# Two gated heads side by side on 64 partitions each: the scores of a forgetting attention, their masks, and a projection cut at 384

## The chip, the core and the metric

One NeuronCore of a Trainium2 chip runs the whole program. The metric is the device time of one execution in microseconds (us); lower is better. The kernel is written by hand for the five engines: TensorE (PE: matmuls; PEld: its weight loads), VectorE (DVE), ScalarE (ACT), GpSimd (POOL) and SyncE (SP, which issues the DMAs).

## The reference, cut to what matters

512 tokens of width 1024 go through a transformer block with a "forgetting" attention, then through two more blocks, one with a differential attention (DA), one with a latent attention (MLA). All is fp32. The parts that the change touches:

```python
# forgetting attention: 8 heads of 64, in four query blocks i of 128
logits = einsum(q[:, :, q0:q1], k[:, :, :q1])             # q times 64 ** -0.5
logits = logits + c[:, :, q0:q1, None] - c[:, :, None, :q1] # c: cumsum of log forget gates
logits = where(s_pos <= t_pos, logits, -inf)              # causal, token by token
p = softmax(logits); out = p @ v[:, :, :q1]
# DA: 8 heads, each with two maps of 64; mask by chunks of 64 tokens
a = p[:, :, 0] - lam * p[:, :, 1]
# MLA: 16 heads; keys of 64 + 32 columns; mask by chunks of 64 tokens
proj = h @ w_in                   # 1024 -> 384 (q latent) + 256 (kv latent) + 32
sc = (einsum(q_nope, k_nope) + einsum(q_pe, k_pe)) * scale
```

## The kernel before

**Numbers as two parts.** Every fp32 operand is split into a high and a low part (tensors `R`, `WH`, `WL`, `KT`, `PT`), and each product is three matmuls: high by high, low by high, high by low.

**Order.** The host program describes each strand of work as a Python generator. `run()` picks the next step again and again: it estimates from `takes()` when each engine is free and when each operand is ready, and emits the step that can begin first. The order it finds is fixed in the program; on the chip each engine works through its own list in that order and waits on semaphores. Weights are loaded by SP into `RAW` (2 buffers), split by ACT (`whi`) and DVE (`wlo`) into 3 slots, and used by `gemm_f` and `gemm_t`.

**Forgetting scores (fg).** Two groups `A0`, `A1` of four heads. `attention(..., "fg", 2)` makes 32 units (head, query block i), of nk = 128, 256, 384 or 512 keys. A unit's step `score` has five matmuls over all 128 partitions (lines 1747 to 1753): three products of 2 heads' queries (128 rows) with one head's keys. `k_tiles` puts each head's keys in the upper or lower 64 rows of a tile of its own, and the other 64 rows are zeros (`k_zero`: 16 memsets on POOL at the start), so that the other head's queries add nothing. The fourth (line 1752) adds the gates: `gate_rows` places high and low parts of c in every fourth row by 4 DMAs, `gate_cq` and `key_row` (one per head, 8) copy them on ACT. The fifth (line 1753) adds the mask: `IDR` (identity) times `MASK_C`. The bank in PSUM then goes through `max` (DVE), `exp` (ACT), `p_one` (DVE), `turn` (PE transposes, line 1664), `hi`/`lo`, and `values` (PE, lines 1659 to 1661).

**DA scores.** `score_two` has both maps of a head: queries and keys of map 0 lie in partitions 0 to 63, those of map 1 in 64 to 127. Each matmul takes 64 partitions (lines 1761, 1763), two after each other into two banks, and so for three products and the mask. There are 32 such steps, one for each head and query block.

**MLA scores.** Sixteen heads of four blocks, 64 units of `score` with 96 partitions and no gate. Their mask matmul (line 1753) is `HALF` times `MASK_H`, both of 128 partitions and 128 columns, where the two halves of the partitions hold the same rows.

**Latents.** `gemm_t(NM.X, 8, 512, ...)` and `gemm_t(NM.X, 8, 160, ...)` make the 672 columns of MLA's first projection: for each of 8 slices of 128 inputs and 4 blocks of tokens, three matmuls of 512 columns, then three of 160 (lines 1688 to 1690). `turn_lat(0..3)` wait for the first four results, `turn_lat(4)`, the squares of the kv latent and `kpe` for all eight.

Of the kernel before, what the change touches and what calls it, by code (L numbers as in the profile page):

```python
# [5 lines left out]
P = 128  # L6
# [13 lines left out]
C_ID, C_MA, C_MC, C_IH, C_ONE = 0, 128, 256, 384, 512  # L20
C_SEL = 640
C_BASE = 648
C_CDA, C_SDA = 650, 682
C_CML, C_SML = 714, 778
C_WF = 842
C_END = 906
# [17 lines left out]
    "vec": {"pe": 1, "act": 1}, "cvec": {"pe": 1, "act": 1}, "consts": {"act": 1}, "k_zero": {"pool": 1}, "blank": {"pool": 1},  # L44
# [5 lines left out]
    "key_row": {"act": 1}, "score": {"pe": 1}, "score_two": {"pe": 1}, "max": {"dve": 1}, "exp": {"act": 1},  # L50
# [87 lines left out]
def takes(kind, eng, f):  # L138
# [9 lines left out]
    if eng == "pe":  # L148
        if kind == "gemm_f":
            return 3 * len(f["xs"]) * mm(512)  # L150
        if kind == "warm":
            return 430.0
        if kind == "gemm_t":
            return 3 * len(f["xs"]) * mm(f["width"])
        if kind == "mix":
            return 3 * mm(512)
        if kind == "score":
            return (3 if f["gate"] is None else 4) * mm((f["i"] + 1) * P) + 62
        if kind == "score_two":
            return 3 * max(220.0, 1.1 * mm((f["i"] + 1) * P)) + 200  # L160
# [36 lines left out]
    return {"acc": 1595.0, "window": 1250.0, "kpe_copy": 1130.0, "k_zero": 520.0, "ramp": 220.0}.get(kind, 120.0)  # L197

def build(nc, a, out):  # L200
    with ExitStack() as ctx:
# [11 lines left out]
        RC = sb("RC", [P, 512], F32R)  # L213
# [17 lines left out]

        IDR, MASK_C, MASK_H, HALF = (RC[:, n * P:n * P + P] for n in range(4))

# [22 lines left out]
        strands, ready_at, free_at = [], {}, dict.fromkeys(LAG, 0.0)  # L256
# [7 lines left out]
        def emit(kind, **fields):  # L264
            t = None
            for eng, n in SIGNALS[kind].items():
# [33 lines left out]
        def run():  # L300
            while strands:
# [22 lines left out]
                s = min((x for x in can if x[1] == eng and x[0] <= t + PATIENCE[eng]), key=lambda x: x[2].rank)[2]  # L324
# [402 lines left out]
        def landing(s, t):  # L727
# [7 lines left out]
        k_zeros = [emit("k_zero", lo=64 if hh % 2 == 0 else 0, i=s * 8 + hh * 2 + x).pool  # L735
                   for s in range(2) for hh in range(4) for x in range(2)]
        kfree = [[k_zeros[-1]] for _ in range(16)]
# [105 lines left out]
        def k_tiles(base):  # L843
            def put(n, bank, done):
                parts, his = [(base + (2 * n + x) * 2, slice(64 * x, 64 * x + 64)) for x in (0, 1)], []
                for i, r in parts:
                    st = yield step("hi", dst=KT[r, i, :], src=bank[r, :], scale=1.0, after=counts([done, kfree[i], kfree[i + 1]]))
                    his.append(st.act)
                for (i, r), hi in zip(parts, his):
                    st = yield step("lo", dst=KT[r, i + 1, :], src=bank[r, :], high=KT[r, i, :], scale=None, from_x=False, after=[hi])  # L850
                    kready[i] = [st.dve]
                return [st.dve]
            return put

# [10 lines left out]
        def attention(groups, kind, lag):  # L865
            nh = 2 if kind == "da" else 4
            krows = 96 if kind == "mla" else P
            mask = (IDR, MASK_C) if kind == "fg" else (HALF, MASK_H)
            units = [(G, h, i) for G in groups for h in range(nh) for i in range(4)]
# [4 lines left out]
            def key_rows(G, h, u):  # L874
                while u > state.scored + 2 or not (flags.consts and G.gated) or not tiles.fr:
                    yield None
                ck = tiles.get()
                st = yield step("key_row", dst=R[:, ck.i, :], src=G.ck, head=G.h0 + h, after=counts([ck.free, G.ck_done]))
                ck.ready = [st.act]
                G.ckh[h] = ck  # L880

            def one_map(L, u, c, b, scored):
                G, h, i = units[u]
                nk, o = (i + 1) * P, u % STN * 8
                nm, z = ST[:, o + c:o + c + 1], ST[:, o + 2 + c:o + 3 + c]
                mx = yield step("max", dst=nm, src=BK[b.i][:, 0:nk], after=[scored])
# [3 lines left out]
                L.p[c], L.p_done[c] = p, ex.act  # L890

            def unit(u):
                G, h, i = units[u]
                nk, maps = (i + 1) * P, 2 if kind == "da" else 1
                while state.scored < u or u > state.turned + lag or not (G.turned and G.gated and flags.consts and h < G.heads):
                    yield None
                ck = None
                if kind == "fg":
                    while h not in G.ckh:
                        yield None  # L900
                    ck = G.ckh[h]
                L = Group()
                L.p, L.p_done = [None] * maps, [None] * maps
                bs = []
                for c in range(maps):
                    b = yield from bank()
                    bs.append(b)
                if kind == "da":
                    q, kidx = G.Q[h], G.kbase + 4 * h
                    st = yield step("score_two", banks=[b.i for b in bs], q=(q.h.i, q.l.i), kidx=kidx, i=i,  # L910
                                    after=counts([*[b.free for b in bs], q.ready, kready[kidx]]))
                    for c, b in enumerate(bs):
                        spawn(one_map(L, u, c, b, st.pe))
                else:
                    (b,) = bs
                    q = G.Q[h // 2 if kind == "fg" else h]
                    kidx = G.kbase + 2 * h
                    gate = None if ck is None else (G.cq.i, ck.i)
                    more = [] if ck is None else [ck.ready, G.cq.ready]
                    st = yield step("score", bank=b.i, q=(q.h.i, q.l.i), kidx=kidx, i=i, rows=krows, gate=gate, mask=mask,  # L920
                                    after=counts([b.free, q.ready, kready[kidx], *more]))
                    spawn(one_map(L, u, 0, b, st.pe))
                state.scored = u + 1
                if i == 3:
                    if kind == "fg":
                        tiles.put(ck, st.pe)
                    if kind != "fg" or h % 2:
                        drop(q, st.pe)
                while None in L.p_done:
                    yield None  # L930
                o = u % STN * 8
                z, rz = ST[:, o + 2:o + 2 + maps], ST[:, o + 4:o + 4 + maps]
                p1 = FS[:, L.p[0].i, 0:nk]
                if maps == 1:
                    st = yield step("p_one", z=z, rz=rz, p=p1, after=L.p_done)
                else:
                    p2, nl = FS[:, L.p[1].i, 0:nk], ST[:, o + 6:o + 7]
                    while G.nlam is None:
                        yield None
                    st = yield step("p_two", z=z, rz=rz, p1=p1, p2=p2, nl=nl, nlam=G.nlam, after=L.p_done)  # L940
                    fsl.put(L.p[1], st.dve)
# [4 lines left out]
                st = yield step("turn", bank=b.i, src=FS[:, L.p[0].i, 0:nk], i=i, odd=odd, after=counts([b.free, st.dve]))  # L946
                state.turned = u + 1
                fsl.put(L.p[0], st.pe)
# [7 lines left out]
            def values(n):  # L956
# [4 lines left out]
                odd = h % 2  # L961
                pair = G.O[h if kind == "da" else h // 2]
# [3 lines left out]
                at_v = h if kind == "da" else h // 2  # L966
                vs = [(G.V[j // 2].h.i, G.V[j // 2].l.i, (j % 2) * 256 + at_v * P) for j in range(4)]
# [3 lines left out]
                if h == nh - 1:  # L971
# [5 lines left out]
                O = BK[b.i]  # L977
                if kind == "da":
                    ev, sq = (yield from fslot()), (yield from fslot())
                    squared = yield step("o_sq", dst=FS[:, sq.i, 0:S], bank=b.i, after=counts([st.pe, sq.free]))  # L980
# [1240 lines left out]
```

## Time and profile before

| | us |
|---|---|
| median of 3 runs | 1829.36 (1827.6 to 1829.54) |
| the profiled execution, whole | 1828.21 |
| its span, from the first to the last instruction | 1826.4 |
| PE busy in the span | 1808.6 (99%), 8960 matmuls |
| DVE / ACT / POOL busy | 1121.5 / 799.3 / 145.2 |

The granted TensorE clock is 0.999 of full speed over the span. The forgetting scores lie between 68 and 141 us, the DA scores between 619 and 797, the latents' projection between 1210 and 1246, MLA's scores between 1270 and 1425. A PE row's duration is longer than the distance to the next one's start, since matmuls overlap: what a matmul costs a full PE is the distance from its start to the start of the next.

### The profile page before, as it was taken

How to read it: one execution, taken by the hardware profiler on the slowest of the kernel's cores; microseconds unless marked ns; L12 is line 12 of the kernel's file. 1: busy time of each engine (PE TensorE's matmuls, PEld its weight loads, DVE VectorE, ACT ScalarE, POOL GpSimd, SP SyncE). 2: the span in 40 equal slices, each digit the busy share in tenths (PEclk: the TensorE clock that was granted, in tenths of full speed). 3: DMA queues.
4: the chain of work that ended last, by engine and by line, in shares of the span. 5: the costliest groups of instructions: out<-in, count | busy, mean ns of one | idle time of the engine just before them, and what ended most of it. 6: DMA issues, size and time to landing. Idle time of an engine off the chain costs nothing.

```text
span 1826.4 us, 23160 instructions
## 1 busy us (share of the span) xinstructions
PE 1808.6 (99%) x8960; PEld 1494.4 (82%) x8960; DVE 1121.5 (61%) x1898; ACT 799.3 (44%) x1426; POOL 145.2 (8%) x149
## 2 busy tenths in 40 slices
PE   9999999999999999999999999999999999999998
PEld 7898788888888888888888888779888888888886
DVE  5577644344345777696754654655989776366375
ACT  6562432122235455544432433447766544144144
POOL 4003200000004100002000000024000100000000
PEclk9999999999999999999999999999999999999999
DMA  5212323322332211213323333222011233332331
GB/s 160 71 36 67 105 92 93 92 93 93 100 96 92 70 59 61 68 58 93 93 93 92 93 93 99 92 79 73 26 58 36 59 93 97 99 93 93 92 117 68
DMA packets 128251, 152.24 MB, mean 83 GB/s; under 512 B 9291, under 2 KB 100973, under 8 KB 128141
## 3 DMA queue, kind: packets, MB, share of 16 engines
q1 hardware_dynamic: 127980, 150.69, 26.8%
q8 instruction: 71, 1.16, 0.3%
q14 instruction: 40, 0.32, 0.1%
q10 hardware_dynamic: 160, 0.07, 0.0%
HBM read 148.56 MB, written 2.10 MB: 82 GB/s over the span
## 4 chain that ended last, share of the span: by engine, by line
PE 92%; DVE 3%; issue 1%; ACT 1%; POOL 1%; DMA 0%; SPq 0%; DVEq 0%; POOLq 0%; ACTq 0%
PE bk L1659 22%; PE bk L1661 22%; PE bk L1660 22%; PE bk L1688 6%; PE bk L1689 5%; PE bk L1690 5%; PE bk L1664 4%; PE bk L1761 1%; PE bk L1747 1%; PE bk L1749 1%; PE bk L1748 1%; PE bk L1726 1%; DVE XT L1821 1%; PE bk L1733 1%; POOL FS L2130 1%
## 5 line engine op out<-in xcount | busy, mean ns | idle before, releaser
L1659 PE MATMUL bk<-R,WH 128*128 128x512 f32 x1764 | 700.6, 397 | 1.8 <-DVE R L1799 1.3
L1660 PE MATMUL bk<-R,WH 128*128 128x512 f32 x1764 | 696.7, 395 | 0.0
L1661 PE MATMUL bk<-R,WL 128*128 128x512 f32 x1764 | 696.7, 395 | 0.0
L1809 DVE TENSOR_TENSOR WL<-RAW,WH 128x1024 fp32r<-128x1024 f32 (+4 forms) x277 | 341.1, 1232 | 529.3 <-ACT WH L1990 527.8
L1990 ACT ACTIVATE WH<-RAW 128x1024 fp32r<-128x1024 f32 (+4 forms) x277 | 287.9, 1039 | 651.6 <-PE bk L1661 593.0
L1659 PEld LDWEIGHTS bk<-R,WH 128*128 128x128 f32 x1764 | 330.8, 188 | 81.7 <-issue 2.9
L1661 PEld LDWEIGHTS bk<-R,WL 128*128 128x128 f32 x1764 | 330.6, 187 | 80.9
L1660 PEld LDWEIGHTS bk<-R,WH 128*128 128x128 f32 x1764 | 330.8, 188 | 78.7
L1688 PE MATMUL bk<-WH,R 128*128 128x512 f32 (+4 forms) x528 | 187.8, 356 | 0.0
L1689 PE MATMUL bk<-WH,R 128*128 128x512 f32 (+4 forms) x528 | 180.2, 341 | 0.0
L1690 PE MATMUL bk<-WL,R 128*128 128x512 f32 (+4 forms) x528 | 180.1, 341 | 0.0
L2130 POOL TENSOR_TENSOR FS<-FS 128x512 f32<-128x512 f32 x49 | 75.4, 1549 | 910.0 <-ACT FS L2014 908.2
L1799 DVE SCALAR_TENSOR_TENSOR FS<-FS,VEC 128x511 f32<-128x511 f32 (+1 forms) x176 | 125.1, 747 | 7.8 <-ACT FS L2096 7.0
L1821 DVE TENSOR_TENSOR XT<-bk,XT 128x512 f32<-128x512 f32 x152 | 100.8, 684 | 25.7 <-PE bk L1661 25.4
L1688 PEld LDWEIGHTS bk<-WH,R 128*128 128x128 f32 x528 | 99.7, 189 | 11.4 <-issue 1.0
L1690 PEld LDWEIGHTS bk<-WL,R 128*128 128x128 f32 x528 | 99.4, 188 | 11.5
L1689 PEld LDWEIGHTS bk<-WH,R 128*128 128x128 f32 x528 | 99.7, 189 | 9.2
L2068 ACT ACTIVATE FS<-bk,SM 128x128 f32<-128x128 f32 (+3 forms) x160 | 83.5, 526 | 52.6 <-DVE SM L1870 52.1
L1910 DVE TENSOR_TENSOR FS<-bk,FS 128x512 f32<-128x512 f32 x136 | 90.2, 685 | 11.1 <-PE bk L1661 9.6
L2096 ACT ACTIVATE FS<-FS,VEC 128x512 f32<-128x512 f32 x88 | 69.0, 810 | 52.7 <-DVE FS L1910 52.7
L1870 DVE TENSOR_REDUCE SM<-bk 128x1 f32<-128x128 f32 (+3 forms) x160 | 72.8, 482 | 6.0 <-PE bk L1753 5.0
L1994 ACT ACTIVATE R<-FS 128x512 fp32r<-128x512 f32 x78 | 47.5, 623 | 63.4 <-DVE FS L1922 43.1
(153 smaller groups left out, 1676.3 us busy)
## 6 DMA issues: line engine op xcount, KB each, us to landing
RAW<-in_ffn_w_up_dram SPq DMA_DIRECT2D x176, 256.0 KB, 3.1
RAW<-in_ffn_w_down_dram SPq DMA_DIRECT2D x44, 512.0 KB, 3.7
RAW<-in_w_gate_dram SPq DMA_DIRECT2D x44, 256.0 KB, 2.9
RAW<-in_w_up_dram SPq DMA_DIRECT2D x44, 256.0 KB, 3.1
RAW<-in_w_down_dram SPq DMA_DIRECT2D x22, 512.0 KB, 3.6
RAW<-in_da_w_qkv_dram SPq DMA_DIRECT2D x32, 256.0 KB, 3.0
RAW<-in_w_out_dram SPq DMA_DIRECT2D x8, 512.0 KB, 3.7
RAW<-in_da_w_qkv_dram SPq DMA_DIRECT2D x8, 512.0 KB, 3.5
```

The costliest lines, as they stand in the source:

```text
L1659: e.matmul(dst, lh, rh, start=start, stop=False)
L1660: e.matmul(dst, lh, rl, start=False, stop=False)
L1661: return e.matmul(dst, ll, rh, start=False, stop=stop)
L1688: e.matmul(dst, R[:, xh, t], wh[:, j, :], start=st.start and j == 0, stop=False)
L1689: e.matmul(dst, R[:, xl, t], wh[:, j, :], start=False, stop=False)
L1690: mm = e.matmul(dst, R[:, xh, t], wl[:, j, :], start=False, stop=st.stop and j == top)
L1799: return e.scalar_tensor_tensor(out=dst, in0=x, scalar=s, in1=y, op0=o0, op1=o1)
L1809: e.tensor_tensor(low, RAW[:, r, 0:m], high.bitcast(F32), ALU.subtract).then_inc(on["wlo_dve"], 1)
L1821: e.tensor_tensor(XT[:, st.m, :], BK[st.bank][:, :], XT[:, st.m, :], ALU.add).then_inc(on["add_dve"], 1)
L1910: e.tensor_tensor(st.dst, BK[st.bank][:, :], st.bc, ALU.mult).then_inc(on["scaled_dve"], 1)
L1990: e.activation(home(st.n)[0], RAW[:, r, 0:m], ACT.Copy).then_inc(on["whi_act"], 1)
L2130: e.tensor_tensor(st.acc, st.acc, st.x, ALU.add).then_inc(on["acc_pool"], 1)
```

## The change

- `fg` and DA now share one function, `paired`. A step `pair` has two heads of the forgetting attention (or the two maps of DA): operands in partitions 0 to 63 and 64 to 127, results in two banks. For the forgetting attention it has three products, the gates as a fourth, and the mask as two matmuls for each side: `UPPER` (queries 0 to 63) by 128 columns and `LOWER` (queries 64 to 127) by 64 columns, since a mask of 128 by 128 does not fit 64 partitions. Keys of two heads stay in one tile (`k_pair` instead of `k_tiles`), so `k_zero` is gone, and there are 4 `key_row` instead of 8.
- The gates' parts are placed for both halves of the partitions: `gate_rows` has 8 DMAs instead of 4.
- `run()` adds 195 ns to a PE step when the kind changes between `pair` and others, and after a `pair` prefers another `pair` that can begin within 200 ns.
- MLA's `score` takes its mask from `UPPER[0:64, :]` and `MASK_H[0:64, :]`, 64 partitions instead of 128. Its three products keep 96.
- The latents' projection is cut at 384 instead of 512: 384 and 288 columns. Three `turn_lat` and the q squares wait for the first four results; two `turn_lat` for the last four.

```diff
-C_ID, C_MA, C_MC, C_IH, C_ONE = 0, 128, 256, 384, 512
+C_ID, C_MA, C_MC, C_IH, C_ONE = 0, 128, 256, 384, 576
...
-        IDR, MASK_C, MASK_H, HALF = (RC[:, n * P:n * P + P] for n in range(4))
+        MASK_C, MASK_H, UPPER, LOWER = RC[:, 0:P], RC[:, P:2 * P], RC[:, 320:448], RC[:, 256:384]
...
+                    if eng == "pe" and (kind == "pair") != tiled[0]:
+                        t += 195.0
+                        tiled[0] = kind == "pair"
...
-                s = min((x for x in can if x[1] == eng and x[0] <= t + PATIENCE[eng]), key=lambda x: x[2].rank)[2]
+                more = [x for x in can if eng == "pe" and tiled[0] and x[2].next[0] == "pair" and x[0] <= t + 200.0]
+                s = min(more or (x for x in can if x[1] == eng and x[0] <= t + PATIENCE[eng]), key=lambda x: x[2].rank)[2]
...
-            chunk(2, 512, (0, wap(m_in, k * P, 2, 0, 512)))
-        for k in (0, 4):
-            chunk(4, 160, (0, wap(m_in, k * P, 4, 512, 160)))
+            chunk(2, 384, (0, wap(m_in, k * P, 2, 0, 384)))
+        for k, n in ((0, 3), (3, 3), (6, 2)):
+            chunk(n, 288, (0, wap(m_in, k * P, n, 384, 288)))
...
+            def bundle(m):
+                n, spec = order[m]
+                G, h = pairs[n]
+                blocks = [i for group in spec for i in group]
+                per = 2 if gated else 1
+                while (state.scored < m or 4 * n + blocks[0] > state.turned // per + lag
+                       or not (G.turned and G.gated and flags.consts) or gated and h not in G.ckh):
+                    yield None
...
                     for r0, src, dst in st.rows:
                         e.dma_start(FS[r0:29 + r0:4, dst, 0:S], R[0:8, src, :].bitcast(F32)).then_inc(s_c, 16)
+                        e.dma_start(FS[64 + r0:93 + r0:4, dst, 0:S], R[0:8, src, :].bitcast(F32)).then_inc(s_c, 16)
...
-                    if st.gate is not None:
-                        cq, ck = st.gate
-                        e.matmul(dst[:, 0:nk], R[:, cq, q], R[:, ck, 0:nk], start=False, stop=False)
-                    e.matmul(dst[:, nk - P:nk], *st.mask, start=False, stop=True).then_inc(on["score_pe"], 1)
...
+                    e.matmul(dst[:, nk - P:nk], UPPER[0:64, :], MASK_H[0:64, :], start=False, stop=True).then_inc(on["score_pe"], 1)
+                elif k == "pair":
+                    for done in st.after:
+                        w.wait_ge(*done)
+                    sides = (slice(0, 64), slice(64, 128))
+                    for i, o, bs in st.parts:
+                        nk, q = (i + 1) * P, slice(i * P, i * P + P)
+                        two = [(r, BK[b][:, o:o + nk]) for r, b in zip(sides, bs)]
+                        for x, y in ((0, 0), (1, 0), (0, 1)):
+                            for r, dst in two:
+                                e.matmul(dst, R[r, st.q[x], q], KT[r, st.kidx + y, 0:nk], start=x == y, stop=False)
+                        if st.gate is None:
+                            for r, dst in two:
+                                mm = e.matmul(dst[:, nk - P:nk], UPPER[r, :], MASK_H[r, :], start=False, stop=True)
+                        else:
+                            cq, ck = st.gate
+                            for r, dst in two:
+                                e.matmul(dst, R[r, cq, q], R[r, ck, 0:nk], start=False, stop=False)
+                            for r, dst in two:
+                                e.matmul(dst[:, nk - P:nk], UPPER[r, :], MASK_C[r, :], start=False, stop=False)
+                            for r, dst in two:
+                                mm = e.matmul(dst[:, nk - 64:nk], LOWER[r, :], MASK_C[r, 0:64], start=False, stop=True)
+                    mm.then_inc(on["pair_pe"], 1)
...
-            yield from gemm_t(NM.X, 8, 512, ev_lat(NM, 0, 512))
-            yield from gemm_t(NM.X, 8, 160, ev_lat(NM, 512, 160))
+            yield from gemm_t(NM.X, 8, 384, ev_lat(NM, 0, 384))
+            yield from gemm_t(NM.X, 8, 288, ev_lat(NM, 384, 288))
```

## Rows read from the trace of the kernel before

**Rows 1.** The page: busy time by engine.

```profile
PE 1808.6 (99%) x8960; PEld 1494.4 (82%) x8960; DVE 1121.5 (61%) x1898; ACT 799.3 (44%) x1426; POOL 145.2 (8%) x149
```

**Rows 2.** Busy time by stretch (from:to, length, engines): MLA's scores.

```profile
1270.00:1430.00 160.00, 156.94 (x969) 139.38 (x970) 142.27 (x344) 107.77 (x280) 12.30 (x18) 1.00 0.13 41
```

**Rows 3.** Timeline of PE (start us, duration us): forgetting scores among other work.

```profile
67.69 0.40 PE L1690 MATMUL bk<-WL,R 128*128 128x512 f32 x1
67.92 0.22 PE L1747 MATMUL bk<-KT,R 128*128 128x128 f32 x1
...
69.81 0.45 PE L1688 MATMUL bk<-WH,R 128*128 128x512 f32 x1
70.10 0.39 PE L1689 MATMUL bk<-WH,R 128*128 128x512 f32 x1
...
77.97 0.40 PE L1690 MATMUL bk<-WL,R 128*128 128x512 f32 x1
...
79.18 0.45 PE L1659 MATMUL bk<-PT,R 128*128 128x512 f32 x1
79.46 0.39 PE L1660 MATMUL bk<-PT,R 128*128 128x512 f32 x1
```

**Rows 4.** Timeline of PE: DA scores, two steps in a row, then one alone.

```profile
733.37 0.40 PE L1690 MATMUL bk<-WL,R 128*128 128x512 f32 x1
733.69 0.55 PE L1761 MATMUL bk<-KT,R 64*128 64x128 f32 x6
734.08 0.28 PE L1763 MATMUL bk<-RC 64*128 64x128 f32 x2
...
734.74 0.50 PE L1688 MATMUL bk<-WH,R 128*128 128x512 f32 x1
735.08 0.40 PE L1689 MATMUL bk<-WH,R 128*128 128x512 f32 x1
...
739.25 0.40 PE L1690 MATMUL bk<-WL,R 128*128 128x512 f32 x1
...
740.36 0.50 PE L1659 MATMUL bk<-PT,R 128*128 128x512 f32 x1
740.70 0.40 PE L1660 MATMUL bk<-PT,R 128*128 128x512 f32 x1
```

**Rows 5.** Timeline of the weight loads at the same place.

```profile
733.69 0.41 PEld L1761 LDWEIGHTS bk<-KT,R 64*128 64x128 f32 x6 [0.37 <-ACT FS L2068]
```

**Rows 6.** Timeline at the mask of one of MLA's units.

```profile
1292.00 0.19 PEld L1753 LDWEIGHTS bk<-RC 128*128 128x128 f32 x1
1292.17 0.23 PE L1753 MATMUL bk<-RC 128*128 128x128 f32 x1
...
1292.24 0.45 PE L1659 MATMUL bk<-PT,R 128*128 128x512 f32 x1
...
1292.52 0.40 PE L1660 MATMUL bk<-PT,R 128*128 128x512 f32 x1
```

**Rows 7.** Timeline of PE: latents' last matmul, then twelve of 384 columns.

```profile
1246.04 0.28 PE L1690 MATMUL bk<-WL,R 128*128 128x160 f32 x1
1246.15 0.37 PE L1688 MATMUL bk<-WH,R 128*128 128x384 f32 x1
...
1248.27 0.60 PE L1664 MATMUL bk<-CN,TOK 128*128 128x128 f32 x4
```

**Rows 8.** Timeline of SP's queue and of ACT: the gates' rows.

```profile
60.31 2.75 SPq L1635 DMA_DIRECT2D FS<-R  x4
...
64.46 0.63 ACT L2086 ACTIVATE R<-FS 128x512 fp32r<-128x512 f32 x1 [3.62 <-DMA FS<-R]
...
66.34 1.32 ACT L2064 ACTIVATE R<-FS,CN 128x512 fp32r<-128x512 f32 x2
```

**Rows 9.** Timeline of POOL at the start.

```profile
1.31 9.18 POOL L2121 MEMSET KT<- 64x512 f32 x16
15.60 1.29 POOL L2130 TENSOR_TENSOR FS<-FS 128x512 f32<-128x512 f32 x1 [5.11 <-ACT FS L2014]
```

More of the change, by code:

```diff
@@ L49 @@
     "rope": {"pool": 3}, "heads": {"pe": 1},
-    "key_row": {"act": 1}, "score": {"pe": 1}, "score_two": {"pe": 1}, "max": {"dve": 1}, "exp": {"act": 1},
+    "key_row": {"act": 1}, "score": {"pe": 1}, "pair": {"pe": 1}, "max": {"dve": 1}, "exp": {"act": 1},
     "p_one": {"dve": 2}, "p_two": {"dve": 4}, "turn": {"pe": 1}, "value": {"pe": 1},
@@ L157, in takes @@
         if kind == "score":
-            return (3 if f["gate"] is None else 4) * mm((f["i"] + 1) * P) + 62
-        if kind == "score_two":
-            return 3 * max(220.0, 1.1 * mm((f["i"] + 1) * P)) + 200
+            return 3 * mm((f["i"] + 1) * P) + 62
+        if kind == "pair":
+            return sum((3 if f["gate"] is None else 4) * mm((i + 1) * P) + (60 if f["gate"] is None else 120) for i, _, _ in f["parts"])
         if kind == "value":
@@ L841, in k_pair @@
             return put
[L843 to L853, printed above, removed]
         def k_tiles64(base):
@@ new lines, in half_out, with normed_out @@
+        def half_out(G, pair, odd, b, done):
+            rows = slice(64 * odd, 64 * odd + 64)
+            lo = yield from halves(R[rows, pair.h.i, :], R[rows, pair.l.i, :], BK[b.i][rows, :], [done], None, pair.h.free + pair.l.free)
+            put_bank(b, lo)
+            pair.half.append(lo)
+            if len(pair.half) == 2:
+                pair.ready = pair.half
+            G.undone -= 1
+            G.done = G.undone == 0
+        def normed_out(G, pair, b, done):
+            ev, sq = (yield from fslot()), (yield from fslot())
+            squared = yield step("o_sq", dst=FS[:, sq.i, 0:S], bank=b.i, after=counts([done, sq.free]))
+            copied = yield step("o_copy", dst=FS[:, ev.i, 0:S], bank=b.i, scale=G.subg, after=counts([done, ev.free]))
+            put_bank(b, squared.act, copied.act)
+            b2 = yield from bank()
+            st = yield step("sums", bank=b2.i, xs=[FS[:, sq.i, 0:S]], after=counts([b2.free, squared.act]))
+            fsl.put(sq, st.pe)
+            r, rooted = yield from root(BK[b2.i][:, 0:4], 4, 1.0 / P, [st.pe])
+            put_bank(b2, rooted)
+            dg = yield from fslot()
+            st = yield step("diag", dst=FS[:, dg.i, 0:S], r=r, after=counts([dg.free, rooted]))
+            b3 = yield from bank()
+            st = yield step("over", bank=b3.i, src=FS[:, dg.i, 0:S], after=counts([b3.free, st.dve]))
+            fsl.put(dg, st.pe)
+            t1 = yield step("o_scale", dst=FS[:, ev.i, 0:S], bank=b3.i, after=[st.pe, copied.act])
+            put_bank(b3, t1.dve)
+            lo = yield from split_pair(pair, FS[:, ev.i, 0:S], [t1.dve])
+            fsl.put(ev, lo)
+            G.undone -= 1
+            G.done = G.undone == 0
@@ L870, in attention @@
+        def attention(groups, lag):
+            units = [(G, h, i) for G in groups for h in range(4) for i in range(4)]
             state = Group()
@@ L872, in attention, with unit @@
             state.halves = {}
[L874 to L882, printed above, removed]
+            def unit(u):
                 G, h, i = units[u]
                 nk, o = (i + 1) * P, u % STN * 8
-                nm, z = ST[:, o + c:o + c + 1], ST[:, o + 2 + c:o + 3 + c]
-                mx = yield step("max", dst=nm, src=BK[b.i][:, 0:nk], after=[scored])
+                while state.scored < u or u > state.turned + lag or not (G.turned and flags.consts and h < G.heads):
+                    yield None
+                nm, z, rz = (ST[:, o + x:o + x + 1] for x in (0, 2, 4))
+                b = yield from bank()
+                q, kidx = G.Q[h], G.kbase + 2 * h
+                st = yield step("score", bank=b.i, q=(q.h.i, q.l.i), kidx=kidx, i=i, rows=96,
+                                after=counts([b.free, q.ready, kready[kidx]]))
+                state.scored = u + 1
+                if i == 3:
+                    drop(q, st.pe)
+                mx = yield step("max", dst=nm, src=BK[b.i][:, 0:nk], after=[st.pe])
                 p = yield from fslot()
@@ L889, in one_map @@
                 put_bank(b, ex.act)
[L890 to L941, printed above, removed]
@@ L942, in unit @@
+                st = yield step("p_one", z=z, rz=rz, p=FS[:, p.i, 0:nk], after=[ex.act])
                 odd = h % 2
@@ L945, in unit @@
                 b = yield from bank()
-                st = yield step("turn", bank=b.i, src=FS[:, L.p[0].i, 0:nk], i=i, odd=odd, after=counts([b.free, st.dve]))
+                st = yield step("turn", bank=b.i, src=FS[:, p.i, 0:nk], i=i, odd=odd, after=counts([b.free, st.dve]))
                 state.turned = u + 1
-                fsl.put(L.p[0], st.pe)
+                fsl.put(p, st.pe)
                 src = BK[b.i][:, 0:nk].rearrange("p (j c) -> p j c", c=P)
@@ L976, in values @@
                         drop(v, st.pe)
[L977 to L980, printed above, removed]
-                    copied = yield step("o_copy", dst=FS[:, ev.i, 0:S], bank=b.i, scale=G.subg, after=counts([st.pe, ev.free]))
-                    put_bank(b, squared.act, copied.act)
-                    b2 = yield from bank()
-                    st = yield step("sums", bank=b2.i, xs=[FS[:, sq.i, 0:S]], after=counts([b2.free, squared.act]))
-                    fsl.put(sq, st.pe)
-                    r, rooted = yield from root(BK[b2.i][:, 0:4], 4, 1.0 / P, [st.pe])
-                    put_bank(b2, rooted)
-                    dg = yield from fslot()
-                    st = yield step("diag", dst=FS[:, dg.i, 0:S], r=r, after=counts([dg.free, rooted]))
-                    b3 = yield from bank()
-                    st = yield step("over", bank=b3.i, src=FS[:, dg.i, 0:S], after=counts([b3.free, st.dve]))
-                    fsl.put(dg, st.pe)
-                    t1 = yield step("o_scale", dst=FS[:, ev.i, 0:S], bank=b3.i, after=[st.pe, copied.act])
-                    put_bank(b3, t1.dve)
-                    lo = yield from split_pair(pair, FS[:, ev.i, 0:S], [t1.dve])
-                    fsl.put(ev, lo)
-                else:
-                    rows = slice(64 * odd, 64 * odd + 64)
-                    lo = yield from halves(R[rows, pair.h.i, :], R[rows, pair.l.i, :], O[rows, :], [st.pe], None,
-                                           pair.h.free + pair.l.free)
-                    put_bank(b, lo)
-                    pair.half.append(lo)
-                    if len(pair.half) == 2:
-                        pair.ready = pair.half
-                G.left -= 1
-                G.done = G.left == 0
+                yield from half_out(G, pair, odd, b, st.pe)
             for G in groups:
-                G.left = nh
-            if kind == "fg":
-                for u in range(0, len(units), 4):
-                    spawn(key_rows(*units[u][:2], u))
+                G.undone = 4
             for n in range(len(units) // 4):
@@ L1329, in turn_lat @@
         def turn_lat(f):
-            while len(lat.toks) < (4 if f < 4 else 8):
+            n = 4 if f < 3 else 8
+            while len(lat.toks) < n:
                 yield None
@@ L1333, in turn_lat @@
             b = yield from bank()
-            st = yield step("heads", bank=b.i, c0=f * P, width=P, after=counts([b.free, lat.toks[0:4 if f < 4 else 8]]))
+            st = yield step("heads", bank=b.i, c0=f * P, width=P, after=counts([b.free, lat.toks[n - 4:n]]))
             lat.ups.append(st.pe)
@@ L1339, in sq_lat @@
         def sq_lat(ssq, c0, width, o):
-            while len(lat.toks) < (4 if c0 == 0 else 8):
+            n = 4 if c0 == 0 else 8
+            while len(lat.toks) < n:
                 yield None
             jk = yield from fslot()
-            free = counts([jk.free, lat.toks])
+            free = counts([jk.free, lat.toks[n - 4:n]])
             for t in range(4):
@@ L1755, in tensor_program @@
                     for done in st.after:
                         w.wait_ge(*done)
-                    nk, q = (st.i + 1) * P, slice(st.i * P, st.i * P + P)
-                    maps = [(slice(64 * c, 64 * c + 64), BK[b]) for c, b in enumerate(st.banks)]
-                    for x, y in ((0, 0), (1, 0), (0, 1)):
-                        for r, dst in maps:
-                            e.matmul(dst[:, 0:nk], R[r, st.q[x], q], KT[r, st.kidx + y, 0:nk], start=x == y, stop=False)
-                    for r, dst in maps:
-                        mm = e.matmul(dst[:, nk - P:nk], HALF[r, :], MASK_H[r, :], start=False, stop=True)
@@ L2062, in scalar_program @@
                         w.wait_ge(*done)
-                    sel = CN[:, C_SEL + st.head:C_SEL + st.head + 1]
+                    sel = CN[:, C_SEL + st.pair:C_SEL + st.pair + 1]
                     e.activation(st.dst, st.src, ACT.Copy, scale=sel).then_inc(on["key_row_act"], 1)
```

198 lines of the change are left out of this document (156 added, 42 removed).

## The prediction

> **What bounds the kernel.** I read the page first. PE is busy for 99% of the span, the other engines for at most 61% [rows 1]. So the time is the length of PE's list of instructions plus its few waits, and the other engines count only where they make PE wait. Then the stretches: in MLA's scores DVE is busy for 142 of 160 us, close behind PE with 157 [rows 2]. PE gets 3 us of idle time there, so there is little that could take in more work. After that I went through PE's timeline with one question: how far apart do neighbouring matmuls start? That distance is the price, not the duration in the row. A matmul of 512 columns shows 0.40 us but costs 0.23, the distance from 67.69 to 67.92 [rows 3]; one of 384 columns costs 0.177, since twelve fill 1246.15 to 1248.27 [rows 7].
>
> The sum is made against the profiled execution, 1828.2 us (span 1826.4, 1.8 outside it). The median of the runs shown is 1829.4, 1.2 more, and I add this at the end.
>
> **Part 1: the forgetting scores as pairs.** Before: from 67.69 to 70.10 lie one matmul of 512 columns, the blocks of 128, 256 and 384 keys of a head, and another matmul of 512 [rows 3]. 2.41 less twice 0.233 leaves 1.94 for the three blocks. From 77.97 to 79.46 the same way: 1.49 less 0.47 is 1.02 for the block of 512 [rows 3]. A head costs 2.96, and eight cost 23.7 us.
>
> After: the nearest rows are DA's, which issue the same 64-partition pairs. Blocks 128 and 256 together: 733.37 to 735.08, less 0.47, is 1.24. Block 384: 739.25 to 740.70, less 0.47, is 0.98 [rows 4]. Block 512 has three passes (a pass is one matmul on each side) that are each 0.233 less 0.177 longer than those of 384: 1.15. Three passes of 384 columns at full-width price are 0.53 of the 0.98, so the two sides do run at the same time, and the rest is a fixed price of about 0.4. Together 3.37 for two maps, with three products and one mask. The gates add a fourth pass: 0.10, 0.12, 0.177 and 0.233, or 0.63. The price for 128 columns is from 733.69 to 734.08, three passes and a start [rows 4]. The second mask matmul, again at the price of a short pass, adds 0.10 four times, 0.4. That is 4.40 for two heads and 17.6 us for eight: **6.1 us saved**. This has 128 and 256 joined and the others alone. If the planner joins nothing the saving is 4.7, if it joins all in twos 7.5.
>
> ACT and DVE lose four `hi` and four `lo` and four `key_row`. They are not the bound here, so this is worth nothing by itself. The 16 memsets on POOL end at 10.5 us, and POOL's next work begins at 15.60 after waiting for ACT [rows 9]: nothing either.
>
> **Part 2: what a change of tiling costs.** The fixed price deserves a look of its own. Block 384 takes 0.98, of which 0.53 are products and 0.06 the mask; the mask's distance to the next start in full width is 1292.17 to 1292.24 [rows 6]. The block of 512 in full width has 1.02 for four products (0.93) and a mask (0.06), so it leaves 0.03 [rows 3]. So to go into a 64-partition stretch and out again costs 0.39 less 0.03, **0.36 us**. The rows show where it lies: the last full matmul starts at 733.37 and the pair at 733.69, 0.09 later than the usual 0.23 [rows 4]; the pair's first weights load starts at 733.69 too, after an idle gap of 0.37 for the loads, while at full width the mask's load at 1292.00 runs ahead of its matmul at 1292.17 [rows 5, 6]. On the way out the next full matmul takes 0.34 to its successor instead of 0.23 [rows 4].
>
> The preference for another `pair` joins some DA stretches. The trace has 24 of them for 32 steps, mostly in the pattern of rows 4. Each one less saves 0.36. I take three, **1 us saved**. Joining needs four free banks, and those of the first step come free only after its `max` and `exp`, so most will stay apart. Bounds: 0 and 2.9 (all eight that could go down to 16).
>
> **Part 3: MLA's mask on 64 partitions.** This edit looks like tidying up, and it carries the sum. Its three products keep 96 partitions, and there was no gap between them and a mask of 128: 0.06 from the mask to the next start, the weights loaded ahead [rows 6]. `UPPER[0:64, :]` has the very shape of line 1763's left side, partitions 0 to 63. So each of 64 units (4 groups, 4 heads, 4 blocks) goes into a 64-partition stretch for one matmul and out again, with nothing beside it on the other 64 partitions. Price 64 times 0.36, 23.0 us. The stage's own PE idle time of 3 us [rows 2] may take in some; I count **21 us lost**. Behind the mask on PE's list stand the transposes and values of earlier units and the weight products, and behind its result DVE's `max`; all of them are just later, since PE is the bound. Bounds: at least the two gaps that are seen directly, 0.09 in and 0.06 out (0.34 less 0.28, the value after a mask at full width, 1292.24 to 1292.52 [rows 6]), 9.6 us. At most a wait until the mask is written, 0.23 [rows 6], in place of 0.06, besides 0.09, a bare weight load of 0.11 and 0.06 after it: 0.43 each, 27.5 us.
>
> The Trainium skill speaks against this edit: in "TensorEngine Tiling (Array Packing)", section "Key Properties", a change of tiling mode (not just of tile) drains the engine. By that rule the mask costs its gap each time, and this trace agrees with about 0.36 us for a way in and out.
>
> **Part 4: the latents.** Before, 96 matmuls of 512 at 0.233 and 96 of 160 at 0.11 (1246.04 to 1246.15 [rows 7]), 22.4 and 10.6: 33.0. After, 96 of 384 at 0.177 less what a first one costs extra, so 0.175, and 96 of 288. The trace has none of 288; between 0.11 and 0.175 I take it in proportion to its columns, 0.131. 16.8 and 12.6: 29.4. **3.6 us saved**, 2 to 5 as that price is nearer to one end or the other. The short matmuls of 160 columns paid for a weight load rather than for their columns; that waste goes. The tail after the projection gets one transpose group more and ACT reads 288 instead of 160 columns, hidden by the next projection's 24 us before the first score at 1270.
>
> **Part 5: the gates come later.** Four DMAs of `gate_rows` take SP 2.75 us to issue, and ACT waits 3.62 us for them until 64.46; `gate_cq` and `key_row` end about 67.0, and PE starts the first score at 67.92 [rows 3, 8]. Eight DMAs land about 2.75 later. The planner still assumes the old 4 us, so it will put the first pair where it was: PE waits until about 69.7. **1.7 us lost**, bounds 0 (other work stands there) and 3. SP's next weight load stands behind them, but PE has up to three split slots ahead, over 10 us of work.
>
> **Sum.** 1828.2 - 6.1 - 1 - 3.6 + 21 + 1.7 = 1840.2; with the 1.2, 1841.4. I say 1841 us.
>
> **Rivals.**
> 1. *A lone 64-partition matmul costs nothing extra* (other side). The gap in rows 4 may belong to pairs alone: the partitions 64 to 127 and their weights. Then MLA loses nothing: 1829.4 - 6.1 - 1 - 3.6 + 1.7 = 1820. For it: the planner's price for `score` does not rise. Against: the first matmul of the pair stands on partitions 0 to 63 and is itself late, with its weights. The edit decides the sign: below about 0.14 us for each mask the change wins. In the Trainium skill, "TensorE: Matmul & The Clock Gate", section "The mechanism", weight loads aimed at the background buffer are pulled ahead of running matmuls; by that rule the mask's load would be hidden and the time would be this rival's. The load at 733.69 [rows 5] is not pulled ahead at such a change. Chance 0.16.
> 2. *DVE sets MLA's stage*, being busy for 89% of it [rows 2], and PE's extra time falls half into waits: 10 us instead of 21, 1831. Against: PE's idle time there is 3 us of 160. Chance 0.08.
> 3. *Each way in and out waits for a full write*, 27.5 us with nothing taken in: 1848. Chance 0.06.
>
> **Numbers.** My forecast has 0.70: its own range 1834 to 1848. Slower by over 0.2% (3.7 us, about what a measurement of this kernel can tell from no change) is the forecast, rival 3 and a part of rival 2: 0.76. Faster is rival 1 and a little of small prices adding up: 0.17. Within: 0.07. With every term at its better bound, and 3 us of the masks taken in by idle time, the sum is 1829.4 - 7.5 - 2.9 - 5 + 9.6 - 3 = 1820.6; with every term at its worse bound 1829.4 - 4.7 - 2 + 27.5 + 3 = 1853.2. The range runs from 1825 to 1850 and leaves out most of rival 1 and the worst sum.
>
> **What would show it.** Right: the same three products, then the MLA mask's row with 64 partitions, its weight load beginning with it and not before, the next start about 0.25 after it instead of 0.06; the stretch of MLA's scores some 20 us longer. Forgetting scores: about six us less between 68 and 141. Latents: a distance near 0.13 for 288 columns. ACT idle for over 6 us before `gate_cq`. Wrong: if the mask's load runs ahead as at 1292.00, rival 1 holds. If PE idles for long before `turn` steps in MLA, the planner's order was upset by late masks, and the loss passes 25 us.

## The result: 1816 us, faster by 0.7%, where 1841 was forecast

The changed kernel takes 1815.97 us (median of 4 runs, 1813.7 to 1818.26) against 1829.45 for the kernel before: ratio 0.9928, 95% interval 0.9911 to 0.9945. The forecast had the wrong sign. Its page has the same shape as before, with 17 us less of PE for 32 more matmuls:

```profile
span 1811.9 us, 23199 instructions
...
PE 1791.7 (99%) x8992; PEld 1499.9 (83%) x8992; DVE 1122.5 (62%) x1895; ACT 791.6 (44%) x1419; POOL 136.2 (8%) x133
```

What the prediction named as the dear edit is there as named. The timeline at one of MLA's masks (answers to [rows 6]; here line 1837 is the third product and 1838 the mask):

```profile
1307.36 0.34 PE L1837 MATMUL bk<-KT,R 96*128 96x384 f32 x1
1307.62 0.18 PEld L1838 LDWEIGHTS bk<-RC 64*128 64x128 f32 x1 [0.25 <-issue]
1307.63 0.33 PE L1838 MATMUL bk<-RC 64*128 64x128 f32 x1
1307.88 0.19 PEld L1747 LDWEIGHTS bk<-R,WH 128*128 128x128 f32 x1
1307.88 0.51 PE L1747 MATMUL bk<-R,WH 128*128 128x512 f32 x1
...
1308.23 0.40 PE L1748 MATMUL bk<-R,WH 128*128 128x512 f32 x1
```

The mask comes 0.27 after a matmul of 384 columns instead of 0.175, its weights are not loaded ahead, the next start is 0.25 later instead of 0.06, and the one after that 0.35 instead of 0.28: 0.09, 0.19 and 0.07 more. Summed over the 64 units in the way of the prediction, MLA's scores went from 39.8 to 59.0 us.

So with 19 us lost in the masks some 33 us were gained elsewhere, where the other edits were to give 9: about 24 must have come from somewhere that no edit touches. They came from everywhere. Two stretches of 200 us in the first FFN, where PE does nothing but 512-column matmuls; the first row is the kernel before, the second the changed one (number of matmuls behind PE's busy time):

```profile
300.00:500.00 200.00, 200.00 (x859) 160.67 (x858) 78.44 (x91) 48.30 (x54) 0.00 (x0) 1.00 0.31 94
```

```profile
300.00:500.00 200.00, 200.00 (x884) 165.71 (x883) 80.80 (x95) 50.72 (x57) 0.00 (x0) 1.00 0.32 98
```

At the same clock of 1.00 PE gets through 884 instead of 859. The distance from start to start is 0.2267 us instead of 0.2333, in some 5200 `gemm_f` matmuls of one and the same code. The new tables changed nothing in that code but where its operands lie: `CN` grew from 906 to 966 columns and `RC` shrank from 512 to 448.
### The profile page after: what moved, and what is told of

The parts are those of the page before. It is cut to its first block, busy times and chain, and to the rows that moved or that the text cites. A ratio compares the mean times of both kernels' runs of the same rounds, so it can differ in the third digit from the quotient of the medians.

```text
span 1811.9 us, 23199 instructions
## 1 busy us (share of the span) xinstructions
PE 1791.7 (99%) x8992; PEld 1499.9 (83%) x8992; DVE 1122.5 (62%) x1895; ACT 791.6 (44%) x1419; POOL 136.2 (8%) x133
## 4 chain that ended last, share of the span: by engine, by line
PE 93%; DVE 3%; ACT 2%; issue 1%; DMA 0%; POOL 0%; SPq 0%; DVEq 0%; ACTq 0%; POOLq 0%
PE bk L1747 23%; PE bk L1749 22%; PE bk L1748 22%; PE bk L1776 5%; PE bk L1778 5%; PE bk L1777 5%; PE bk L1752 4%; PE bk L1848 2%; PE bk L1838 1%; PE bk L1814 1%; PE bk L1835 1%; PE bk L1821 1%; DVE XT L1917 1%; PE bk L1836 1%; PE bk L1837 1%
## 5 line engine op out<-in xcount | busy, mean ns | idle before, releaser
L1747 PE MATMUL bk<-R,WH 128*128 128x512 f32 x1764 | 693.9, 393 | 3.0 <-DVE R L1895 1.9
L1749 PE MATMUL bk<-R,WL 128*128 128x512 f32 x1764 | 688.5, 390 | 0.0
L1748 PE MATMUL bk<-R,WH 128*128 128x512 f32 x1764 | 688.3, 390 | 0.0
```

The lines of the kernel that those rows point to most:

```text
L1747: e.matmul(dst, lh, rh, start=start, stop=False)
L1748: e.matmul(dst, lh, rl, start=False, stop=False)
L1749: return e.matmul(dst, ll, rh, start=False, stop=stop)
```

## The experiments

The theories after the first reading. A: the place of `R` by itself (modulo 64 or 128) sets what a matmul costs. B: the shorter distance comes from something in the changed kernel's order or clock. C, formed after the second set: what counts is how `R` lies relative to `WH` and `WL`, one of which is loaded while the other is streamed.

**First set: the place and the mask, each with and without.** "Moved" is one edit, `MLA's mask on 128` the other:

```diff
-        CN = sb("CN", [P, C_END], F32)
+        CN = sb("CN", [P, C_END + 8], F32)
```

```diff
-  UPPER[0:64, :], MASK_H[0:64, :], start=False, stop=True).then_inc(on["score_pe"], 1)
+  UPPER, MASK_H, start=False, stop=True).then_inc(on["score_pe"], 1)
```

The kernel before, moved:

> The kernel before with 8 unused fp32 columns behind its constants, so that the tensors R, KT and PT lie 32 bytes further on: they start at a multiple of 64 bytes, as they do in the changed kernel, and nothing else differs. Theory A (the place of the operands in SBUF sets what a matmul costs): the distance between 512-column matmuls falls from 0.233 us to about 0.227, and with 6000 of them the time to 1829 - 33, near 1796 us. Theory B (the distances fell in the changed kernel because of something in its order or its clock): within 0.2% of the kernel before, 1826 to 1833.

The changed kernel, moved back:

> The changed kernel with the same 8 unused columns, so that R, KT and PT start 32 bytes past a multiple of 64, as in the kernel before. Theory A: the gain of the place is gone, 1816 + 33, near 1849 us, so that the change itself comes out slower by about 20. Theory B: still near 1816.

The changed kernel, mask on 128 partitions:

> The changed kernel with MLA's mask back on 128 partitions (the same constants, all their rows). If a lone 64-partition matmul costs a way in and out, about 0.30 us in 64 places as the two traces say, 1816 - 19, near 1797 us. If the longer distances around it are only moved waits, near 1816.

Both:

> MLA's mask on 128 partitions and R, KT and PT 32 bytes past a multiple of 64: the rest of the change without the mask and without the place. Theory A and the mask's price add up: near 1830, the kernel before less the 8 us that pairs and latents were to save, plus what the gates' wait costs, so 1822 to 1830. Theory B: near 1797.

| | us | ratio to before, 95% |
|---|---|---|
| before, moved | 1807.33 | 0.9879 (0.9865 to 0.9894) |
| changed, moved back | 1843.50 | 1.0077 (1.0062 to 1.0092) |
| changed, mask on 128 | 1793.66 | 0.9809 (0.9794 to 0.9823) |
| changed, mask on 128, moved back | 1826.51 | 0.9980 (0.9970 to 0.9990) |

B falls: eight unused columns make the old kernel 22 us faster, and the change at the old place is slower by 0.8%, at 1843.5, where 1841 was forecast. The mask costs 22 us at one place and 17 at the other. But A as put has a hole: the old kernel gained 22 and not 33, with `R` at a multiple of 64.

**Second set: which place.** The kernel before with 24 columns instead of 8:

> The kernel before with 24 unused columns behind its constants: R, KT and PT start at a multiple of 128 bytes, as in the changed kernel (in the run with 8 columns they stood 64 past one). Theory A1 (the place modulo 128 counts: the 512-column distance was 0.233 at 32, 0.229 at 64, 0.227 at 0): 1829 less 6000 times 0.0066, less KT and PT, so about 1791 to 1797 us. Theory A2 (modulo 64 counts and the rest of the changed kernel's distance has another cause): 1807, as with 8 columns.

The changed kernel with the mask on 128 and 16 columns:

> The changed kernel with MLA's mask on 128 partitions and 16 unused columns: R, KT and PT at 64 past a multiple of 128. Theory A1: distance 0.229 instead of 0.227, so 1794 + 11 to 14, about 1806 us. Theory A2: 1794.

The same with the weights' tensors moved:

```diff
+        PADA = sb("PADA", [P, 8], F32)
         WH = sb("WH", [P, NSP, SLOT], F32R)
         WL = sb("WL", [P, NSP, SLOT], F32R)
+        PADB = sb("PADB", [P, 24], F32)
         CN = sb("CN", [P, C_END], F32)
```

> The same with WH and WL 32 bytes past a multiple of 128, while R, KT and PT stay at a multiple. In 5200 of the 512-column matmuls WH and WL are the stationary side, in 750 the moving side. If only the moving side's place counts, the 750 lose 0.0066 each and the time is 1794 + 5, about 1799 us; if the stationary side counts as well, the 5200 lose too, up to 1794 + 39.

They gave 1824.16 us (0.9969, 0.9958 to 0.9980), 1804.53 (0.9856, 0.9839 to 0.9874) and 1825.76 (0.9979, 0.9969 to 0.9989). The first refutes A1 and A2 alike: a multiple of 128, even of 256, and hardly any gain. Ordered by `R` less `WH` modulo 256 the values fall in line: 0, 64, 128 and 32 give 0.2269, 0.2290, 0.2324 and 0.2333 us on average. The third run, meant to part the moving from the stationary side, moved `R` as well and so cannot do that; its difference is 96, with 0.2333. It does clear the table: in this run alone `CN` moved with `R` (65792 and 102912, a difference of 0 modulo 256) and not with `WH`, and the short distance did not come.

**Third set: theory C against A.** All tensors by 32 bytes, then by 128 (a pad ahead of `XT`, the first tensor), then those behind the constants alone by 256 and by 192:

> The changed kernel with MLA's mask on 128 partitions, and all tensors, weights and R alike, 32 bytes further on. Theory C (what counts is how far the two operands that are read at the same time lie from each other, modulo some 256 bytes: R less WH is 0 mod 256 in the changed kernel, 32 in the kernel before): the distance stays 0.227 us, the time 1794. Theory A (R's own place counts: it is now at 32 past a multiple of 64, as in the kernel before): 0.233 and 1826.

> All tensors 128 bytes further on; R starts at 102912 as in the run of the kernel before with 24 columns, where the distance was 0.232. Theory C: 0.227 and 1794. Theory A with a period of 256 bytes: 0.232 and about 1821.

> Only the tensors behind the constants move, by 256 bytes. With a period of 256 bytes, in either theory, 1794. With a longer one the distance changes: toward 0.213 if R and the weights 256 apart were still in each other's way, or up.

> Only the tensors behind the constants move, by 192 bytes: R less WH is 192 mod 256. If the distance is symmetric around 0 (64 gave 0.229), 0.229 and 1805; if it follows the step away from 0 in one direction (0: 0.227, 64: 0.229, 128: 0.232), 0.235 and about 1835.

And the kernel before with 56 columns, so that it has difference 0 as well:

> The kernel before with 56 unused columns: R less WH is 0 mod 256 bytes, as in the changed kernel. Theory C: distance 0.2267, so 1829.5 less about 32 to 34, near 1797 us; the changed kernel's 1816 would then be 19 slower than the kernel before at the same place, and 3 faster with MLA's mask on 128 partitions. Were something in the changed kernel's order needed for 0.2267, it would stay above 1805.

The same 200 us of the first FFN in five runs, one row each: all tensors by 32; all by 128; `R` by 192; the kernel before moved by 32 (difference 64); the kernel before moved by 224 (difference 0).

```profile
300.00:500.00 200.00, 200.00 (x884) 165.58 (x884) 80.62 (x93) 50.73 (x57) 0.00 (x0) 1.00 0.31 97
```

```profile
300.00:500.00 200.00, 200.00 (x884) 165.62 (x883) 80.62 (x93) 50.74 (x57) 0.00 (x0) 1.00 0.31 97
```

```profile
300.00:500.00 200.00, 200.00 (x859) 161.12 (x857) 77.93 (x91) 48.13 (x54) 0.00 (x0) 1.00 0.31 95
```

```profile
300.00:500.00 200.00, 200.00 (x875) 164.28 (x874) 81.60 (x95) 50.14 (x57) 0.00 (x0) 1.00 0.31 95
```

```profile
300.00:500.00 200.00, 200.00 (x884) 165.63 (x883) 82.09 (x96) 50.73 (x58) 0.00 (x0) 1.00 0.31 97
```

| `R` less `WH`, mod 256 | matmuls in 200 us | runs, us |
|---|---|---|
| 0 | 884 | before 1797.99; mask on 128: 1793.66, all moved by 32: 1795.75, by 128: 1795.72, `R` by 256: 1794.91 |
| 32 | 859 | before 1829.96; mask on 128: 1826.51 |
| 64 | 875 and 876 | before 1807.33; mask on 128: 1804.53 |
| 96 | 859 | mask on 128: 1825.76 |
| 128 | 862 | before 1824.16 |
| 192 | 859 | mask on 128: 1825.28 |

Theory C holds in all of them. `R` at 102816 gives 859 next to a `WH` at 41088 and 884 next to one at 41120; `R` at 102912 gives 862 next to 41088 and 884 next to 41216. The period divides 256, and it is not symmetric around 0 (64 gives 875, 192 gives 859).

The traces hold a sharper test, for `gemm_t` has the two sides the other way round: it streams `WH` and `WL` and loads `R`. If the address of the streamed operand less that of the loaded one is what counts, then 64 and 192 change places there. The first and the last of 54 `gemm_t` matmuls in a row, at a clock of 1.00, first with `R` less `WH` at 64 (mask on 128, 16 columns), then at 192:

```profile
569.73 0.39 PE L1776 MATMUL bk<-WH,R 128*128 128x512 f32 x1
...
582.09 0.40 PE L1778 MATMUL bk<-WL,R 128*128 128x512 f32 x1
```

```profile
577.46 0.40 PE L1776 MATMUL bk<-WH,R 128*128 128x512 f32 x1
...
589.61 0.39 PE L1778 MATMUL bk<-WL,R 128*128 128x512 f32 x1
```

53 distances take 12.36 and 12.15 us: 0.2332 at 64, where `gemm_f` has 0.2290, and 0.2292 at 192, where `gemm_f` has 0.2333. At 0 they are 0.2268. So the difference counts from the streamed to the loaded operand of the matmul itself. Traffic of other engines or DMAs at `R`, `WH` and `WL` does not change sides in this way, and so it does not explain the distances.

**One part of the change at a time.** MLA's mask alone in the kernel before:

```diff
-  mask = (IDR, MASK_C) if kind == "fg" else (HALF, MASK_H)
+  mask = (IDR, MASK_C) if kind == "fg" else (HALF[0:64, :], MASK_H[0:64, :])
```

> The kernel before with only MLA's mask changed to 64 partitions (the same two constants, their first 64 rows). The prediction's part 3: 64 times 0.36 less what idle time takes in, 1829 + 21, about 1850 us; bounds 1839 and 1857. The rival that a lone 64-partition matmul costs nothing: 1829.

1847.86 us, 1.0098 (1.0082 to 1.0114): 18 us lost, inside the bounds and 3 under the value taken. The rival that it costs nothing is out.

On the changed kernel with the mask on 128, first the latents' cut undone, then the gates, then the planner's preference:

```diff
-            yield from gemm_t(NM.X, 8, 384, ev_lat(NM, 0, 384))
-            yield from gemm_t(NM.X, 8, 288, ev_lat(NM, 384, 288))
+            yield from gemm_t(NM.X, 8, 512, ev_lat(NM, 0, 512))
+            yield from gemm_t(NM.X, 8, 160, ev_lat(NM, 512, 160))
```

> The changed kernel with MLA's mask on 128 partitions and the latents' projection cut at 512 again. By the prediction's part 4 the cut at 384 saves 3.6 us of PE: 1794 + 3.6, about 1797 to 1798. If PE's new wait of 2.6 us at 1235 (ACT waiting for the late roots of the squares) and the half clock behind it come from the cut, they eat the saving: 1793 to 1795.

```diff
-            ready_at[id(s_c), 144] = at_time(bases[1]) + 4000.0
+            ready_at[id(s_c), 144] = at_time(bases[1]) + 6900.0
```

> The changed kernel with MLA's mask on 128 partitions, and the planner told that the gates' eight DMAs land 6.9 us after their bases instead of 4.0. It then places the first pair later and PE's wait of 1.8 us at 68 goes: 1794 - 1.8, about 1792, and another 1.7 less where a half clock followed that wait. If the order of the rest is upset, within 2 us of 1794 either way.

```diff
-                        t += 195.0
+                        t += 0.0
...
-                more = [x for x in can if eng == "pe" and tiled[0] and x[2].next[0] == "pair" and x[0] <= t + 200.0]
+                more = []
```

> The changed kernel with MLA's mask on 128 partitions, without the 195 ns in the plan and without the preference for a further pair. The trace after has 25 stretches of pairs in DA where the kernel before had 24, so the preference joined nothing there: theory says within 1.5 us of 1794. If it did join some of the forgetting scores, 0.36 us more for each that falls apart.

1794.26 us (1792.49 to 1794.97), 1792.02 (1791.13 to 1795.11) and 1798.37 (1798.08 to 1798.92), beside 1793.66 (1793.12 to 1797.18) for their common base. Three more kernels with the same list of work and the same difference of 0 (third set) gave 1794.91 to 1795.75, so a difference of one or two us between medians of four or five runs is not clear of the spread. The cut at 384 brings nothing that these runs can tell: its gain is given back. The gates' wait is worth about 1.6 by the medians, which is within this spread. The third expectation missed: without preference and surcharge DA has 29 stretches of pairs instead of 25 and costs 28.8 us instead of 26.7, and PE waits 2.26 us before 821.85, where the base does not: 4.4 of the 4.7, which is clear of the spread. The planner's two lines, taken out together here, are worth more than the pairs they join.

Together, the mask on 128 partitions, the cut at 512 and the gates told:

> MLA's mask on 128 partitions, the latents cut at 512 and the gates' landing told to the planner. Alone, the cut at 512 gave 1794.3 and the gates 1792.0, where the common base gave 1793.7. If both waits go together: 1790 to 1792. If the waits are given back elsewhere: 1794.

1790.09 us (1789.44 to 1790.22), ratio 0.9783 (0.9770 to 0.9796): the best of all, 26 us under the changed kernel. Both waits, the one for the gates and the one behind the latents, are gone from its trace.

## Why the prediction was wrong, step by step

**The step that failed** stands in its first paragraph and under every term: that a 512-column matmul costs 0.23 us, "the distance from 67.69 to 67.92 [rows 3]", after the change as before it. I took the untouched 6000 matmuls as a constant and read the shift of `CN` and `RC` in the diff as bookkeeping. No rival spoke of it. With the difference at 0 instead of 32 the matmuls cost 0.2267: the kernel before gains 32 us by that alone (1829.96 to 1797.99). At an equal place the sum comes out near the forecast of plus 12.0: moved back, the changed kernel is at 1843.50, 13.6 over the kernel before. In part that is luck, because two misses cancel. Without the masks the change was to save 9.0 and saved 3.4 (1829.87 to 1826.51), and the masks were to cost 21 and cost 17.0 (1826.51 to 1843.50).

**The forgetting scores as pairs** (6.1 saved): right. In the run without the gates' wait they cost 18.1 us against 17.6 forecast and 23.7 before. A pair of blocks 128 and 256 in the changed kernel, the four gate and mask kinds in between (answers to [rows 4]):

```profile
83.46 0.40 PE L1778 MATMUL bk<-WL,R 128*128 128x512 f32 x1
83.79 0.55 PE L1848 MATMUL bk<-KT,R 64*128 64x128 f32 x6
84.18 0.27 PE L1855 MATMUL bk<-R 64*128 64x128 f32 x2
84.28 0.28 PE L1857 MATMUL bk<-RC 64*128 64x128 f32 x2
84.40 0.25 PE L1859 MATMUL bk<-RC 64*128 64x64 f32 x2
84.48 0.60 PE L1848 MATMUL bk<-KT,R 64*128 64x256 f32 x6
...
85.27 0.50 PE L1776 MATMUL bk<-WH,R 128*128 128x512 f32 x1
```

The gate pass is 0.10, as taken, the two masks 0.12 and 0.08.

**The way in and out, 0.36 us**: right in kind, large by a fifth. From the 64 units it is 0.30: 0.33 where a 512-column matmul follows, 0.29 to 0.32 where transposes do. **DA's joined stretches** (1 saved): 25 stretches instead of 24, 26.7 us instead of 27.1, so 0.4. **MLA's mask** (21 lost): 22, 17 and 18 in three comparisons, 19.2 by the traces' distances. The 22 hold two more stretches at half clock than their base (see the last section).

**The latents** (3.6 saved): the price was right, the "hidden" tail was not. The 96 matmuls of 288 columns stand 0.133 apart, 0.131 forecast. But the stage behind them lost it. PE waits for ACT, which waited for the roots of the squares. Of the five small DVE steps that make them, three take about a microsecond each while POOL copies:

```profile
1237.78 0.60 PE L1752 MATMUL bk<-CN,TOK 128*64 128x128 f32 x4 [2.56 <-ACT TOK L2146]
```

```profile
1227.51 1.00 DVE L1934 TENSOR_TENSOR SM<-SM 128x8 f32<-128x8 f32 x1
1228.55 0.17 DVE L1936 TENSOR_TENSOR SM<-SM 128x8 f32<-128x8 f32 x1
1228.75 0.91 DVE L1938 TENSOR_SCALAR SM<-SM 128x8 f32<-128x8 f32 x1
...
1231.10 1.01 DVE L2051 TENSOR_SCALAR SM<-SM 128x4 f32<-128x4 f32 x1
```

That this wait belongs to the cut is shown, since it is gone with the cut at 512. That POOL's copies stretch the DVE steps is not shown by itself, but the same run bears on it: there POOL is idle from 1228.5 to 1232.5, and the same five DVE steps, from 1230.89 to 1232.42, take 0.16 to 0.17 each.

**The gates** (1.7 lost): right to a tenth. ACT waits 6.26 us, and PE starts its first pair at 69.75, forecast 69.7 (answers to [rows 8]):

```profile
67.22 0.63 ACT L2182 ACTIVATE R<-FS 128x512 fp32r<-128x512 f32 x1 [6.26 <-DMA FS<-R]
...
68.70 0.71 ACT L2160 ACTIVATE R<-FS,CN 128x512 fp32r<-128x512 f32 x1
```

```profile
69.75 0.55 PE L1848 MATMUL bk<-KT,R 64*128 64x128 f32 x6 [1.80 <-ACT R L2160]
```

Of the rivals none came true; 1820 of the first is near 1816 only by chance, since its reason, a mask that costs nothing, is false by all three comparisons. What adds up, in us: place -32.0, everything but the mask at the new place -4.3 (1797.99 to 1793.66), the mask +22.3. Each is the difference of two medians in a chain, so that they must add up, to -14.0; in its own session the result was -13.5. What the prediction lacked is the first term, and of the -4.3 it had promised -9.0.

The Trainium skill says in "TensorEngine Tiling (Array Packing)", section "Key Properties", that a change of tiling mode drains the engine. The runs agree that such a change has a price, 0.30 us for a way in and out; that a drain is what the time goes to, no trace shows.

## What to carry to other kernels

Before a diff's edits are costed, write down the addresses of the large operands before and after it: a table that grows by a few columns moves everything behind it, and in a kernel that is one long list of matmuls this can outweigh every edit. To compare two versions fairly, pad them to the same addresses. Then a matmul on 64 partitions should stand in company or not at all: use all 128 partitions with rows to spare, if its neighbours do.

## What the runs showed of the hardware that was not expected

- The distance of fp32r matmuls of 512 columns, weights loaded alongside, follows the address of the streamed operand less that of the loaded one, modulo 256 bytes: in `gemm_f` 0.2267 us at 0, 0.229 at 64, 0.232 at 128, 0.2333 at 32, 96 and 192. `gemm_t`, with the sides the other way round, gives 0.2333 at 224 (the kernel before, `R` less `WH` 32) and 0.234 at 160 (the weights moved, 96). Whether the two reads meet in the same part of SBUF, as this suggests, no run shows. `R` less `KT` and `R` less `PT` were 0 in every run, so those pairs were not tried.
- A matmul on 96 partitions among those on 128 costs no way in and out: in the run with the mask on 128 it starts 0.226 to 0.236 us after one of 512 columns, the usual distance, where a pair on 64 starts about 0.32 after it.
- The granted clock can be 0.50 (1.2 GHz) for a stretch of 3.4 us. In the changed kernel one begins at 71.0, after PE's wait before 69.75: 16 matmul records lie in it and 26 in the 3.6 us behind it, and a matmul of 512 columns stands 0.42 from the next:

```profile
71.00:74.40 3.40, 3.40 (x16) 2.30 (x12) 2.03 (x9) 2.41 (x9) 0.00 (x0) 0.50 0.49 154
74.40:78.00 3.60, 3.60 (x26) 3.12 (x27) 2.13 (x7) 1.78 (x4) 0.00 (x0) 1.00 0.00 0
```

```profile
72.42 0.63 PE L1778 MATMUL bk<-WL,R 128*128 128x512 f32 x1
72.84 0.63 PE L1776 MATMUL bk<-WH,R 128*128 128x512 f32 x1
```

  The changed kernel's trace has four such stretches before its end, the kernel before none, the run with the mask on 128 two, and the fastest run (1790.09) one. By the two distances, 0.42 and 0.227, such a stretch costs PE about 1.6 us, an estimate; four are over 6 us, and no term of the prediction had them. They may be much of the 5.6 us that the rest of the change saved less than forecast. Which waits are followed by one differs between programs with the same list of work, and each trace is one execution, so their share in a difference of medians stays open.
